# Pooling layer of a four-layer decoder step: loads and weight splits placed in the MLP ahead, cache columns copied on the scalar engine, low parts one block later

## The reference, cut to what matters

```
def mixer_c(h, prefix, n_valid, w_grp, scale):
    xp = concatenate([prefix, h], axis=1)          # prefix: zeros, or 15 cached rows
    for gi, w in enumerate((2, 4, 8, 16)):         # four groups of 256 channels
        tot = sum of the last w rows of xp
        cnt = min(w, t + 1 + n_valid)
        diffs.append(tot / cnt - h)
    y = einsum('btgc,gce->btge', d, w_grp) * scale # one 256 x 256 matrix for each group
    return y, xp[:, T:]                            # the last 15 rows are the new cache
...
x = x + mixer_c(rmsnorm(x, norm1[2]), ...)
x = x + square(relu(rmsnorm(x, norm2[2]) @ w1)) @ w2
```

## Time and profile before

| what | value |
|---|---|
| median of 3 runs | 3104.5 us (3098.15 to 3109.02) |
| profiled execution, device time | 3110.35 us |
| its span in the trace | 3108.5 us |
| PE busy | 2924.0 us, 94% of the span |
| DVE busy | 1418.2 us, 46% |
| ACT busy | 931.0 us, 30% |
| POOL busy | 616.4 us, 20% |
| pooling layer, last `x` of the MLP ahead to first matmul of the next MLP | 1834.5 to 1918.5 us |

### The profile page before, as it was taken

One profiled execution on the slowest core, in us unless ns is written; L12 is line 12 of the kernel. 1 busy time (PEld: TensorE's weight loads), 2 busy tenths in 40 slices (PEclk: granted clock), 3 DMA queues, 4 the chain that ended last, 5 costly groups with the idle time before them and its releaser, 6 DMA issues.

```text
span 3108.5 us, 55325 instructions
## 1 busy us (share of the span) xinstructions
PE 2924.0 (94%) x24181; PEld 2800.0 (90%) x24181; DVE 1418.2 (46%) x1950; ACT 931.0 (30%) x1636; POOL 616.4 (20%) x518
## 2 busy tenths in 40 slices
PE   7998899999999899989999975999999988999998
PEld 6997599999999888879999975999999984999998
DVE  4554343344676434344344347343355543443432
ACT  5554222222233412122222222222235543322223
POOL 0001241122210111014122233122130011322213
PEclk9998899999999978669999986999999998999999
DMA  4236424333323000222333321334342345243333
GB/s 121 67 91 192 123 89 129 125 123 124 102 71 85 22 2 2 72 65 90 129 124 124 123 87 52 124 124 124 122 128 64 90 140 173 76 135 119 121 126 101
DMA packets 440936, 318.49 MB, mean 102 GB/s; under 512 B 17181, under 2 KB 427470, under 8 KB 438359
## 3 DMA queue, kind: packets, MB, share of 16 engines
q1 hardware_dynamic: 430967, 277.19, 29.5%
q0 software_dynamic: 9728, 37.75, 3.9%
HBM read 299.62 MB, written 71.68 MB: 119 GB/s over the span
## 4 chain that ended last, share of the span: by engine, by line
PE 84%; DVE 7%; ACT 3%; DMA 2%; issue 2%; SPq 1%; POOL 0%; ACTq 0%; DVEq 0%; POOLq 0%
PE acc L210 68%; PE misc L1667 1%; PE misc L1565 1%; PE misc L1678 1%; PE misc L887 1%; PE acc L1705 1%; PE acc L1698 1%; PE acc L1760 1%; ACT a_sw L1080 1%; PE misc L833 1%; ACT a_p L1036 1%; DMA s_kv<-cache_a_kv 1%; PE acc L1720 1%; PE misc L1682 1%; PE misc L1782 1%
## 5 line engine op out<-in xcount | busy, mean ns | idle before, releaser
L210 PE MATMUL acc<-act_hi,w_hi 128*128 128x272 f32 x3856 | 817.5, 293 | 21.7 <-DVE act_lo L260 13.8
L210 PE MATMUL acc<-act_hi,w_lo 128*128 128x272 f32 x3856 | 802.7, 290 | 0.0
L210 PE MATMUL acc<-act_lo,w_hi 128*128 128x272 f32 x3856 | 802.3, 289 | 0.0
L195 DVE TENSOR_TENSOR w_lo<-w_raw,w_hi 128x1024 fp32r<-128x1024 f32 (+1 forms) x367 | 583.3, 1589 | 314.2 <-ACT w_hi L188 312.8
L210 PEld LDWEIGHTS acc<-act_hi,w_hi 128*128 128x128 f32 x3856 | 608.1, 190 | 30.0 <-issue 18.9
L210 PEld LDWEIGHTS acc<-act_lo,w_hi 128*128 128x128 f32 x3856 | 609.8, 190 | 0.0
L210 PEld LDWEIGHTS acc<-act_hi,w_lo 128*128 128x128 f32 x3856 | 609.3, 190 | 0.0
L188 ACT ACTIVATE w_hi<-w_raw 128x1024 fp32r<-128x1024 f32 (+1 forms) x367 | 388.0, 1057 | 725.7 <-PE acc L210 663.6
L210 PE MATMUL acc<-h_hi,w_hi 128*128 128x272 f32 x2048 | 425.5, 289 | 0.0
L210 PE MATMUL acc<-h_lo,w_hi 128*128 128x272 f32 x2048 | 422.4, 287 | 0.0
L210 PE MATMUL acc<-h_hi,w_lo 128*128 128x272 f32 x2048 | 421.9, 287 | 0.0
(11 more groups left out here) (362 smaller groups left out, 2596.4 us busy)
## 6 DMA issues: line engine op xcount, KB each, us to landing
w_raw<-mlp_w SPq DMA_DIRECT2D x256, 512.0 KB, 3.9
new_a_kv_s<-cache_a_kv SPq DMA_DIRECT2D x128, 381.0 KB, 4.5
s_kv<-cache_a_kv POOLq DMA_DIRECT2D x40, 768.0 KB, 7.8
w_raw<-a_w_in SPq DMA_DIRECT2D x54, 512.0 KB, 4.1
w_raw<-b_w_in SPq DMA_DIRECT2D x32, 512.0 KB, 4.1
w_raw<-a_w_out SPq DMA_DIRECT2D x16, 576.0 KB, 4.0
s_kv<-cache_a_kv POOLq DMA_DIRECT2D x32, 192.0 KB, 5.0
new_a_kv_s<-cache_a_kv SPq DMA_DIRECT2D x16, 372.0 KB, 4.6
```

Of the source, the lines that this page charges most:

```text
L195: nc.vector.tensor_tensor(w_lo[:, t.slot, 0:t.kt, :], w_raw[:, t.raw, 0:t.kt, :], w_hi[:, t.slot, 0:t.kt, :].bitcast(F32), ALU.subtract).t ...
L210: last = nc.tensor.matmul(acc[:, t.first % 2, s, 0:HALF], w[:, t.slot, k, :], a[:, k, s * HALF:(s + 1) * HALF], start=(k == 0 and i == 0), ...
```

## The change

Three loads of the pooling layer, and the split of its weights, move into the MLP ahead: SP issues the loads ahead of weight tile 20 (`sp_ahead`), ACT writes one piece of `c_w_hi` in each of tiles 32 to 39 (`act_ahead`), DVE one piece of `c_w_lo` in each of tiles 40 to 47 (`dve_ahead`). So that the three buffers don't share memory with the MLP's, an unused tensor `c_gap` pushes them behind the MLP's place. The 47 columns of the new cache go to a small buffer of their own, `c_new`, copied by ACT (two instructions in each block), with the sample columns first; PE transposes from there, and DVE's wait for `c_tail_T` is gone. DVE's low part of block `k - 1` is written behind the difference of block `k` (`low`), PE's `products` of a group follow the transpose of the next even block, and `add_to_x` and the gains come one block later.

```
@@ sp_mlp, act_mlp, dve_mlp
             for p in range(2, MLP_TILES + 2):
+                if p == 20 and pool_next(l):
+                    mixers[2].sp_ahead(sp, l + 1)
                 sp_weights(sp, WeightTile("mlp", l, p))
...
                 act_split(act, WeightTile("mlp", l, p + 2))
+                if pool_next(l) and 32 <= p < 32 + KD:
+                    mixers[2].act_ahead(act, p - 32)
...
                 dve_split(dve, WeightTile("mlp", l, p + 2))
+                if pool_next(l) and 40 <= p < 40 + KD:
+                    mixers[2].dve_ahead(dve, p - 40)
@@ MixC
+            @staticmethod
+            def sp_ahead(sp, l):
+                sp.wait_ge(evac_done, base["mlp", l - 1] + 8)
                 sp.dma_start(c_prev[:, :], aps["state_c_pool"][0].rearrange("b j d -> (b j) d")).then_inc(c_landed, 16)
                 sp.dma_start(c_inv[:, :, :], aps["c_pool_inv"]).then_inc(c_landed, 16)
                 sp.dma_start(c_w_raw[:, :, :], aps["c_w"][0].rearrange("g (k p) e -> p (g k) e", p=P)).then_inc(c_landed, 16)
+            @staticmethod
+            def act_ahead(act, k):
+                act.wait_ge(c_landed, 48)
+                nc.scalar.activation(c_w_hi[:, k, :], c_w_raw[:, k, :], ACT.Copy).then_inc(c_wh, 1)
+            @staticmethod
+            def dve_ahead(dve, k):
+                dve.wait_ge(c_wh, k + 1)
+                nc.vector.tensor_tensor(c_w_lo[:, k, :], c_w_raw[:, k, :], c_w_hi[:, k, :].bitcast(F32), ALU.subtract).then_inc(c_w_ready, 1)
@@ pe
                     pe.wait_ge(c_h, k + 1)
+                    pe.wait_ge(c_copied, KD + 2 * k + 2)
                     nc.tensor.transpose(misc[2 + k // 4][0:TAIL, (k % 4) * P:(k % 4 + 1) * P],
-                                        c_d[:, k % 2, 0:TAIL], ident[:, :]).then_inc(c_tail_T, 1)
-                    if k % 2:
-                        products(k // 2)
+                                        c_new[:, k % 2, :], ident[:, :]).then_inc(c_tail_T, 1)
+                    if k >= 2 and k % 2 == 0:
+                        products(k // 2 - 1)
+                products(KD // 2 - 1)
@@ act
                 for k in range(KD):
+                    act.wait_ge(c_h, k + 1)
+                    if k >= 2:
+                        act.wait_ge(c_tail_T, k - 1)
+                    nc.scalar.activation(c_new[:, k % 2, 0:NS].rearrange("p (b t) -> p b t", t=DEC_T),
+                                         c_x[:, k, CP:].rearrange("p (b j) -> p b j", j=CS)[:, :, PRE:], ACT.Copy).then_inc(c_copied, 1)
+                    nc.scalar.activation(c_new[:, k % 2, NS:TAIL], c_x[:, k, CP - PRE:CP], ACT.Copy).then_inc(c_copied, 1)
                     act.wait_ge(c_d_done, k + 1)
                     nc.scalar.activation(act_hi[:, k, :], c_d[:, k % 2, :], ACT.Copy).then_inc(c_d_hi, 1)
-                    if k % 2 == 0 and k:
-                        gains_of(k - 2)
+                    if k % 2 and k >= 3:
+                        gains_of(k - 3)
@@ dve, block k
-                    nc.vector.tensor_copy(c_d[:, b, 0:PRE], cur[:, CP - PRE:CP])
-                    nc.vector.tensor_copy(c_d[:, b, PRE:TAIL].rearrange("p (b t) -> p b t", t=DEC_T),
-                                          cur[:, CP:].rearrange("p (b j) -> p b j", j=CS)[:, :, PRE:]).then_inc(c_h, 1)
...
-                    dve.wait_ge(c_tail_T, k + 1)
...
-                    if k == 0:
-                        for j in range(KD):
-                            dve.wait_ge(c_wh, j + 1)
-                            nc.vector.tensor_tensor(c_w_lo[:, j, :], c_w_raw[:, j, :], c_w_hi[:, j, :].bitcast(F32), ALU.subtract).then_inc(c_w_ready, 1)
-                    dve.wait_ge(c_d_hi, k + 1)
-                    nc.vector.tensor_tensor(act_lo[:, k, :], c_d[:, b, :], act_hi[:, k, :].bitcast(F32), ALU.subtract).then_inc(c_d_ready, 1)
-                    if k % 2 == 0 and k:
-                        add_to_x(k - 2)
-                    elif k >= 3:
-                        for j in (k - 3, k - 2):
+                    if k >= 1:
+                        low(k - 1)
+                    if k % 2 and k >= 3:
+                        add_to_x(k - 3)
+                    elif k >= 4:
+                        for j in (k - 4, k - 3):
                             dve_gain(dve, 2 * l + 1, j)
+                low(KD - 1)
+                for k in (KD - 4, KD - 3):
+                    dve_gain(dve, 2 * l + 1, k)
                 add_to_x(KD - 2)
                 for k in (KD - 2, KD - 1):
                     dve_gain(dve, 2 * l + 1, k)
```

More of the change, by code:

```diff
@@ L343, in cache_copy, with pool_next @@
                          old[bass.ds(b, 1), first + DEC_T:first + DEC_T + rows, :]).then_inc(caches_copied, 16)
+        def pool_next(l):
+            return l + 1 in layers and (l + 1) % 3 == 2
         def sp_mlp(sp, l):
             for p in range(2, MLP_TILES + 2):
+                if p == 20 and pool_next(l):
+                    mixers[2].sp_ahead(sp, l + 1)
                 sp_weights(sp, WeightTile("mlp", l, p))
@@ L485, in build_step @@
             c_d = lsb("c_d", [P, 2, TOK])
+            c_tail = lsb("c_tail", [TAIL, D])
+            lsb("c_gap", [P, (68352 - 4 * (KD * CW + 2 * CW + 2 * TOK + D)) // 4])
             c_w_raw = lsb("c_w_raw", [P, KD, 256])
@@ L490, in build_step @@
             c_inv = lsb("c_inv", [P, len(WINDOWS), 16])
-            c_tail = lsb("c_tail", [TAIL, D])
-        c_landed, c_zero, c_prev_T, c_prev_done = sem("c_landed"), sem("c_zero"), sem("c_prev_T"), sem("c_prev_done")
+            c_new = lsb("c_new", [P, 2, TAIL])
+        c_landed, c_zero, c_prev_T, c_copied = sem("c_landed"), sem("c_zero"), sem("c_prev_T"), sem("c_copied")
         c_h, c_wh, c_d_done, c_d_hi, c_d_ready, c_w_ready = (sem("c_h"), sem("c_wh"), sem("c_d_done"), sem("c_d_hi"),
@@ L500, in sp @@
             @staticmethod
-            def sp(sp, l):
-                place_free(sp, l)
+            def sp_ahead(sp, l):
+                sp.wait_ge(evac_done, base["mlp", l - 1] + 8)
                 sp.dma_start(c_prev[:, :], aps["state_c_pool"][0].rearrange("b j d -> (b j) d")).then_inc(c_landed, 16)
@@ L505, in sp @@
                 sp.dma_start(c_w_raw[:, :, :], aps["c_w"][0].rearrange("g (k p) e -> p (g k) e", p=P)).then_inc(c_landed, 16)
+            @staticmethod
[7 more added lines that the diff above has]
+            @staticmethod
+            def sp(sp, l):
+                place_free(sp, l)
                 sp.dma_start(aps["new_c_pool_s"][0, :, 0:PRE - DEC_T, :], aps["state_c_pool"][0, :, DEC_T:PRE, :]).then_inc(c_stored, 16)
                 sp.wait_ge(c_tail_done, 2)
-                sp.dma_start(aps["new_c_pool_p"][0, 0], c_tail[0:PRE, :]).then_inc(c_stored, 16)
+                sp.dma_start(aps["new_c_pool_p"][0, 0], c_tail[NS:TAIL, :]).then_inc(c_stored, 16)
                 for b in range(DEC_B):
                     sp.dma_start(aps["new_c_pool_s"][0, b, PRE - DEC_T:PRE, :],
-                                 c_tail[PRE + b * DEC_T:PRE + (b + 1) * DEC_T, :]).then_inc(c_stored, 16)
+                                 c_tail[b * DEC_T:(b + 1) * DEC_T, :]).then_inc(c_stored, 16)
                 sp.wait_ge(c_stored, 16 * (2 + DEC_B))
@@ L535, in products @@
                         pe.wait_ge(c_w_ready, KD)
-                        pe.wait_ge(c_prev_done, KD)
+                        pe.wait_ge(c_copied, KD)
                     for o in (2 * g, 2 * g + 1):
@@ L565, in act @@
                                          acc[:, k // 4, 0, (k % 4) * P:(k % 4) * P + PREV_ROWS].rearrange("p (b j) -> p b j", j=PRE),
-                                         ACT.Copy).then_inc(c_prev_done, 1)
+                                         ACT.Copy).then_inc(c_copied, 1)
                 act_norm_R(act, 2 * l)
-                for k in range(KD):
-                    nc.scalar.activation(c_w_hi[:, k, :], c_w_raw[:, k, :], ACT.Copy).then_inc(c_wh, 1)
                 def gains_of(first):
@@ L590, in dve @@
                 dve.wait_ge(c_zero, 2)
-                dve.wait_ge(c_prev_done, KD)
+                dve.wait_ge(c_copied, KD)
                 row = gain_row(2 * l)
@@ L598, in add_to_x, with low @@
                                                        gains[:, 2 * DEPTH + 1, o:o + 1], halves(x[:, o, :]), ALU.mult, ALU.add).then_inc(pool_x, 1)
+                def low(k):
+                    dve.wait_ge(c_d_hi, k + 1)
+                    nc.vector.tensor_tensor(act_lo[:, k, :], c_d[:, k % 2, :], act_hi[:, k, :].bitcast(F32), ALU.subtract).then_inc(c_d_ready, 1)
                 for k in range(KD):
@@ L606, in dve @@
                                                    ALU.mult, ALU.mult)
-                    chain(dve, nc.vector.scalar_tensor_tensor(
+                    nc.vector.scalar_tensor_tensor(
                         cur[:, CP:].rearrange("p (b j) -> p b j", j=CS)[:, :, PRE:], x[:, k, SEQ:TOK].rearrange("p (b t) -> p b t", t=DEC_T),
```

(6 more changed lines are left out.)

## The result

The changed kernel takes **3087.52 us** (median of 8 runs, 3072.62 to 3093.56) against 3107.19 us for the kernel before (8 runs, 3098.15 to 3111.02). The ratio is 0.993, with a 95% interval of 0.9911 to 0.995: faster by some 20 us. The profiled execution took 3072.62 us, with a span of 3070.8 us, and is the fastest of the eight. It may not be set against the profile of before by its span: of the 37.7 us between the two spans (3108.5 and 3070.8) less than half belong to the change, as the next table shows.

The account below looks back on a forecast made before the run. PE bounds the MLP ahead; the pooling layer is bound by a load, then DVE block by block. Head 4.1 + loop 15.5 - end 2.6 = 17.0 us, off the median 3104.5: 3087.5 us, range 3080 to 3096.

Parts of the forecast that it names:

- The head: Pooling layer up to DVE's first scaling: with loads long done, PE's transposes follow the norm's sums, gaining 4.1 us.
- The upper bound: Head: if earlier transposes keep 2.4 GHz, R comes at about 1841.7, a gain of 5.4 us.
- The loop: DVE's first scaling to block 7's last difference: 49.2 us instead of 64.7, a gain of 15.5 us.
- The second reckoning: Loop gain summed from what goes (weight split, copies, waits, work moved behind the loop): 16.6 us.
- The removed copies: Loop: DVE's copies priced at 0.17 us each, not their mean; POOL's stall passes to the next shifted sum.
- The end: Behind the last difference: MLP begins 1.7 us later, plus 0.9 us of PE stall for POOL's sum; 2.6 us lost.
- The bounds of 1.0 and 4.5 us: The range given for the loss at the end, around 2.6 us.
- The MLP ahead: MLP before the pooling layer: the moved loads and weight split fit into idle time and cost nothing.
- The handshake (1): Rival, loop: late ACT high parts or PE transposes bring 5.0 + 2.0 us of waits back, 3094.5 us; chance 0.08.
- Stalls that go with the copies (2): Rival, loop: POOL's stalls vanish with DVE's copies, 3.0 us more gained, 3084.5 us; chance 0.08.
- PE entering the MLP at half clock (3): Rival, next MLP: a whole first tile at 1.2 GHz costs 6.0 us more, 3093.5 us; chance 0.06.
- The wait for the loads (4): Rival, MLP ahead: ACT's wait for loads at tile 32 delays weight splits and PE; slower, 3117 us; chance 0.04.

Follow-up runs that it names:

- e5_again: The changed kernel once more, without an edit, for a second profile; median 3086.49 us of 6 runs, ratio 0.9935 to the kernel before.
- e6_nosums: The changed kernel with POOL's squares and sums for the next norm cut from 544 columns to 16; profiled execution 3085.65 us.
- e8_tail: The changed kernel with block 7's low part put between the additions of outputs 4 and 5; profiled execution 3082.47 us.
- e1_loads: The kernel before with only the three pooling loads moved into the MLP ahead; profiled execution 3102.95 us.
- e3_cols: The kernel before with only the cache columns copied by ACT into their own buffer and DVE's wait for PE's transpose gone; profiled execution 3098.44 us.
- e2_low: The kernel before with only the order changed: low parts and all behind them one block later; profiled execution 3085.26 us.
- e7_actsq: e8_tail with the squares taken by ACT, so that POOL only adds; median 3078.5 us of 4 runs, ratio 0.9908 to the kernel before.

## Why the prediction was right

The time came out at 3087.52 where 3087.5 was predicted. That closeness is partly luck. The prediction started from 3104.5, the median of three runs; with eight runs it is 3107.19. The stage gained 18.0 instead of 17.0 us (17.2 in e5_again), and medians of this kernel move by a few microseconds. What held is the working, step by step.

**Which number to subtract from.** The prediction took the gain from the median of the runs shown, because the work taken away has a fixed length. Had it been read off one profile against another, the change would have looked like 37.7 us. The layers that the change does not touch account for the other 19.7: the delta-rule layer 10.7, the second attention layer 7.6 and the first 1.9, less 0.5 that the first MLP took longer. For the delta-rule layer e5_again shows that the same kernel also takes the longer time, and for the second attention layer e5_again, e6_nosums and e8_tail do; that the granted clock is the cause is suggested by the traces and not shown. The first attention layer and its norm's sums end at 427.3 us in after and at 423.6 to 428.8 in the other profiles that hold the whole change, against 429.2 before.

**The head (4.1 predicted, 3.75 measured).** The step was right that the transposes follow the sums; e1_loads shows the loads as the only cause. The missing 0.35 us is in what comes behind: from the sums' end (1825.76 + 1.21) to `R` at 1831.21 go 4.24 us where 3.92 were counted. PE waits 0.22 for `diag`, which was counted at nothing, and the broadcast takes 2.66 instead of about 2.06, at half clock to its end. The 3.92 were called the row at the lower clock, but they were not that throughout: in the kernel before the clock rose during the broadcast (0.50 until 1846.5, 0.96 from there to 1847.0), and its last two matmuls took 0.40 us instead of 0.58:

```profile
1846.64 0.40 PE L318 MATMUL misc<-diag,ones 32*128 32x32 f32 x2
```

The upper bound, transposes and broadcast at 2.4 GHz throughout, did not come: only the transposes were partly at full clock (1.43 instead of 1.86). In e5_again, with the clock at half from the sums on, the head gained 2.9 us and not 3.75.

**The loop (49.2 predicted, 48.39 measured).** The eight blocks without POOL were summed to 32.6 us; they are 2.75, 2.73, twice 3.64, twice 4.54 and twice 5.42, together 32.68. The step between two blocks, counted at 0.82 and with a pair at 2.20, is about 0.85 and 2.12 (1855.37 to 1857.49), all seven together 10.3 instead of 10.6. The term that was sized too high is POOL: 6.0 predicted, 5.4 by e6_nosums, since block 6 was stalled by 3.2 us and not 3.4, and block 4, with three POOL instructions, by 2.2 and not 2.6. The second reckoning, from what goes (16.6), was nearer than the smaller one that was kept (15.5).

**The removed copies.** That a copy which takes a stall must be priced without it was right in the main: e3_cols gained 3.73 us, not 6.4. Most of the stall passes to the shifted sums behind it (2.5 of 3.0 us), though not to the next one, as counted, but to those after it: the first sum of block 7 takes 0.87 us in e3_cols. The rule of the Trainium skill that the prediction named (SBUF — State Buffer, Who interferes with whom) agrees with these rows: DVE and POOL take turns there, and without POOL's work (e6_nosums) blocks 4 and 6 are as short as 5 and 7. The copy has one SBUF input, so the rule as quoted, for two inputs, does not cover it; that it stood still as well is what its 1.11 us show.

**The end (2.6 predicted, 2.0 measured).** The mechanism was right: POOL's squares and sums, started 1.59 us behind the last difference (1.55 predicted), become the last thing, which e8_tail shows by moving PE and gaining nothing. The stall of PE was counted at 0.9 us and is 0.24; the MLP's first matmul was counted at 7.7 us and comes at 7.33, held by the addition of output 6, because PE's last 18 products ran partly at full clock (3.31 us instead of 4.34). The bounds of 1.0 and 4.5 us had no working: the times named beside them, 13.7 and 15 us, give 1.7 and 3.0.

**The MLP ahead (0 predicted, 0.0 measured)** repeats to 0.01 us, with PE at 48.00 of 48. The loads took longer beside the MLP's own stream, 8.5 us for `c_w_raw` instead of 7.0, which nobody waited for.

**The rivals.** The handshake (1) is gone: in the kernel after DVE waits for ACT nowhere in the loop, since nothing stands idle ahead of a low part. e2_low, without the copies moved, shows what it would have looked like, 1.9 us in block 3. Stalls that go with the copies (2) are refuted by e3_cols but for some 0.5 us. PE entering the MLP at half clock (3) did not occur in the kernel after, whose first pairs of the MLP take 0.52 and 0.41 us, the latter as in the MLP's steady part. The variants show how near it is: in e6_nosums and e7_actsq the clock rises only behind the products, and in e8_tail it fell behind the MLP's first tile. The wait for the loads (4) had nothing to wait for: 8.5 us against the 96 at which it would have begun to cost and the 113 at which the gain would have been gone. (The 3117 us given for it belong to loads 30 us beyond the 96; 30 us beyond the 113 it would be some 3134.)

## What to carry to other kernels

Cut a trace at events that both kernels have and compare stage by stage; the difference between two spans held 19.7 us here from stretches that the change does not touch. On an engine that works in order, price a block by a neighbouring block of the same form, and the cost of another engine's work by the difference between blocks with and without it: both held here to 0.6 us or better. When a small instruction looks dear because it sits where another engine blocks it, removing it gives back little more than its own length (most of the stall passes on, 2.5 of 3.0 us here); to get the stall back, the blocking work has to go or shrink.

## What the runs showed of the hardware that I had not expected

The MLP ahead repeats from run to run to 0.01 us (386.33 from norm to norm, or 387.2 in four of the ten; the 0.86 more are the norm's sums at the lower clock, and from sums to sums all ten have 386.23), while the delta-rule layer, in which PE is busy for some 227 of 250 us, takes 619 to 635 us with a mean granted clock of 0.83 to 0.88. And the clock decides a stretch as short as the head: in e5_again it had fallen before the norm's sums, which then took 2.06 us instead of 1.21, and the head was 10.35 instead of 9.53.

```profile
1836.31 2.06 PE L288 MATMUL misc<-ones,sumsq 128*128 128x1 f32 x10 [3.39 <-POOL sumsq L276]
```
